# Modulation blocks of a conditioned decoder layer: eight products on TensorE against weighed sums on VectorE

## What is computed

```python
cond = jax.nn.silu(c)                                  # 1024 values
mod = (cond @ w_ada[l] + b_ada[l])[:, None, :]         # w_ada: 1024 x 6144
sh_m, sc_m, g_m, sh_f, sc_f, g_f = jnp.split(mod, 6, axis=-1)
h = modulate(rms_norm(x, norm_mix_g[l]), sh_m, sc_m)
x = x + g_m * hybrid_mixer(h, w_in[l], ...)            # w_in: 1024 x 7168, w_out: 1024 x 1024
h = modulate(rms_norm(x, norm_ffn_g[l]), sh_f, sc_f)
y = moe_ffn(h, router_w[l], router_b[l], w_gate_up[l], b_gate_up[l], w_down[l], b_down[l])
x = x + g_f * y
return rms_norm(x, final_norm_g)
```

## Time and profile before

| | us |
|---|---|
| median of 3 runs | 1220.74 (1220.02 to 1222.51) |
| profiled execution | 1220.39 |
| its span, first to last instruction | 1218.6 |
| mean granted TensorE clock, share of full | 0.951 |

### The profile page before, as it was taken

One profiled execution on the slowest core, in us unless ns is written; L12 is line 12 of the kernel. 1 busy time (PEld: TensorE's weight loads), 2 busy tenths in 40 slices (PEclk: granted clock), 3 DMA queues, 4 the chain that ended last, 5 costly groups with the idle time before them and its releaser, 6 DMA issues.

```text
span 1218.6 us, 23737 instructions
## 1 busy us (share of the span) xinstructions
PE 976.9 (80%) x9347; PEld 517.7 (42%) x9348; DVE 449.8 (37%) x1115; ACT 400.4 (33%) x773; POOL 8.6 (1%) x21
## 2 busy tenths in 40 slices
PE   6999999988688888997568997568898678656565
PEld 3788989853244333443124443112443123111122
DVE  0655654654244234442123444222344224222223
ACT  1544424424233234432123334222344224222223
POOL 0200000000000000000000000000000000000000
PEclk9999999999999999999889999987999789898898
DMA  9979487789999989999998869999989999999995
GB/s 353 377 277 347 170 320 293 298 353 427 425 425 426 426 357 429 426 426 426 426 426 363 348 273 425 427 426 429 424 338 426 428 424 429 424 428 425 426 426 224
DMA packets 60354, 467.50 MB, mean 384 GB/s; under 512 B 5148, under 2 KB 6468, under 8 KB 24484
## 3 DMA queue, kind: packets, MB, share of 16 engines
q1 hardware_dynamic: 60324, 467.06, 93.0%
HBM read 466.00 MB, written 1.05 MB: 383 GB/s over the span
## 4 chain that ended last, share of the span: by engine, by line
PE 47%; DMA 25%; SPq 18%; issue 4%; DVE 4%; ACT 1%; DVEq 0%; ACTq 0%
PE B L1213 23%; DMA W<-in_w_down_dram 21%; PE B L960 15%; SPq L367 13%; SPq L369 4%; DMA W<-in_w_gate_up_dram 4%; PE B L1222 3%; PE B L980 2%; PE B L1164 1%; DVE EW L896 1%; DVE EW L899 1%; DVE EW L893 1%; DMA raw<-in_w_ada_dram 1%; ACT EW L592 1%; PE B L987 1%
## 5 line engine op out<-in xcount | busy, mean ns | idle before, releaser
L1213 PE MATMUL B<-W,mT 128*32 128x256 f32 (+1 forms) x5888 | 550.5, 518 | 150.8 <-DMA W<-in_w_gate_up_dram 113.5
L1213 PEld LDWEIGHTS B<-W,mT 128*32 128x32 f32 x5888 | 213.7, 113 | 458.6 <-DMA W<-in_w_gate_up_dram 177.4
L602 ACT ACTIVATE hT<-hT 32x256 bf16<-32x256 bf16 x368 | 152.6, 415 | 237.4 <-DVE hT L913 229.5
L893 DVE TENSOR_SCALAR EW<-B 128x256 f32<-128x256 f32 x46 | 19.5, 424 | 419.6 <-PE B L1213 419.6
L592 ACT ACTIVATE EW<-EW 128x256 f32<-128x256 f32 x46 | 19.2, 417 | 365.5 <-DVE EW L893 365.5
L960 PE MATMUL B<-hh,wh 128*128 128x256 f32 x384 | 110.0, 286 | 0.0
L960 PE MATMUL B<-hl,wh 128*128 128x256 f32 x384 | 108.7, 283 | 0.0
L960 PE MATMUL B<-hh,wl 128*128 128x256 f32 x384 | 108.7, 283 | 0.0
L675 DVE TENSOR_TENSOR wl<-raw,wh 128x2048 fp32r<-128x2048 f32 x32 | 72.8, 2313 | 72.7 <-ACT wh L487 72.7
L1222 PE MATMUL B<-b_gu,mT 128*32 128x512 f32 x368 | 50.5, 601 | 59.7 <-issue 48.4
L487 ACT ACTIVATE wh<-raw 128x2048 fp32r<-128x2048 f32 x32 | 59.6, 1907 | 111.7 <-DMA raw<-in_w_in_dram 76.9
(11 more groups left out here) (216 smaller groups left out, 728.2 us busy)
## 6 DMA issues: line engine op xcount, KB each, us to landing
W<-in_w_gate_up_dram SPq DMA_DIRECT2D x128, 2048.0 KB, 32.6
W<-in_w_down_dram SPq DMA_DIRECT2D x63, 2048.0 KB, 25.5
raw<-in_w_in_dram SPq DMA_DIRECT2D x13, 2048.0 KB, 8.8
raw<-in_w_ada_dram SPq DMA_DIRECT2D x12, 2048.0 KB, 12.2
raw<-in_w_out_dram SPq DMA_DIRECT2D x2, 2048.0 KB, 9.9
raw<-in_w_in_dram SPq DMA_DIRECT2D x2, 1024.0 KB, 11.5
W<-in_w_down_dram SPq DMA_DIRECT2D x2, 1024.0 KB, 38.8
x_sb<-in_x_dram SPq DMA_DIRECT2D x1, 1024.0 KB, 5.0
```

Source lines behind the costliest of these rows:

```text
L602: A(ys[CAP * m:CAP * m + CAP, g * QC:(g + 1) * QC], yp[CAP * g:CAP * g + CAP, m, :], ACT.Copy).then_inc(y_moved, 1)
L1213: t = M(o, src[:, k % KQ, CAP * (k // KQ):CAP * (k // KQ) + CAP], w, start=(first and k == 0), stop=(k == KT - 1))
```

## The change

Blocks i = 1 and 2 (eight of them) leave TensorE. VectorE multiplies each with its condition values, one per partition, and adds it up in a new tile `weighed` (128 x 4 x 512): two instructions per block, a tensor_scalar or scalar_tensor_tensor and a scalar_tensor_tensor. `weigh(1 + h, n)` stands behind the work on bank 0 of section n, and its end is what `ada_used` now counts for these units. TensorE then sums over the partitions with a tile of ones, four matmuls (`sum_weighed`) per half, behind the second spatial step of section U_; `cond` is overwritten with ones after the opening. The fourth opening block goes to the place of `wh[1]`, which is unused then, and is issued without a wait; the ring's places shift by one behind it, so that the first expert units land in other places; ScalarE's first split into `wh[1]` waits for that block's use. The filler transposes ahead of the second opening block are gone.

```diff
+        weighed = sb("weighed", [P, 4, HALF])
...
-        PLACE = (1, 2, 8, 0, 3, 4, 5, 6, 7, 9)
+        PLACE = (0, 1, 8, 2, 3, 4, 5, 6, 7, 9)
...
+        ASIDE = 3
+
+        def place(n):
+            return n if n < ASIDE else n - 1
+
         def raw_slot(n):
-            return raw[:, (n % RING) * UW:(n % RING + 1) * UW]
+            if n == ASIDE:
+                return slot(5)
+            return raw[:, (place(n) % RING) * UW:(place(n) % RING + 1) * UW]
+
+        def landed(n):
+            if n == ASIDE:
+                return s_aside, 16
+            return s_slot[place(n) % RING], 16 * (place(n) // RING + 1)
...
             for n, (kind, s, h) in enumerate(units):
-                if n >= RING:
-                    m = n - RING
+                if n != ASIDE and place(n) >= RING:
+                    m = n - RING if n - RING > ASIDE else n - RING - 1
...
             split_high(0, (1,))
+            act.wait_ge(ada_used, 4)
             split_high(1)
...
-                dve.wait_ge(ada_used, 4 * (i + 1))
+                if i == 0:
+                    dve.wait_ge(ada_used, 4)
+                else:
+                    dve.wait_ge(ada_summed, i)
...
             add_bias(0)
+            V.memset(cond[:, 0, :], 1.0).then_inc(ones_ready, 1)
...
+            def weigh(i, q):
+
+                n = unit_no[("ada", i, q)]
+                dve.wait_ge(*landed(n))
+                if q == 0 and i > 1:
+                    dve.wait_ge(ada_summed, i - 1)
+                w = raw_slot(n).rearrange("p (k j n) -> p k j n", k=2, j=4)
+                if q == 0:
+                    step(V.tensor_scalar(weighed[:, :, :], w[:, 0], cT[:, 0:1], None, ALU.mult))
+                else:
+                    step(V.scalar_tensor_tensor(weighed[:, :, :], w[:, 0], cT[:, 2 * q:2 * q + 1], weighed[:, :, :], ALU.mult, ALU.add))
+                V.scalar_tensor_tensor(weighed[:, :, :], w[:, 1], cT[:, 2 * q + 1:2 * q + 2], weighed[:, :, :], ALU.mult, ALU.add).then_inc(ada_used, 1)
+                dve.wait_ge(ada_used, 4 * i + q + 1)
+                if q == 3:
+                    dve.nop().then_inc(weighed_ready, 1)
...
+                        if b == 0 and n < 4:
+                            weigh(1 + h, n)
...
+            def sum_weighed(i):
+
+                if i == 1:
+                    pe.wait_ge(v_gelu, TA * NH)
+                    pe.wait_ge(ones_ready, 1)
+                if i == 2:
+                    pe.wait_ge(mod_ready, 2)
+                pe.wait_ge(weighed_ready, i)
+                for j in range(4):
+                    t = M(B[7][32 * j:32 * j + 32, :], cond[:, 0, :], weighed[:, j, :], start=True, stop=True)
+                t.then_inc(ada_summed, 1)
...
             for q in range(1, 4):
-                keep_warm(WARM_LOAD, B[5])
+                if q > 1:
+                    keep_warm(WARM_LOAD, B[5])
                 modulation(0, q)
...
-                        if b == 0 and i < 4:
-                            modulation(1 + h, i)
                     if s == U_:
                         spatial(2 * h + 1)
+                        sum_weighed(1 + h)
```

More of the change, by code:

```diff
@@ L221, in hybrid_trunk @@
         ranks = B[4][:, 0:3 * E]
-        s_x = sem("s_x"); s_rows = sem("s_rows"); s_bada = sem("s_bada"); s_bada_rest = sem("s_bada_rest"); s_first = sem("s_first"); s_gffn = sem("s_gffn")
+        s_x = sem("s_x"); s_rows = sem("s_rows"); s_bada = sem("s_bada"); s_bada_rest = sem("s_bada_rest"); s_first = sem("s_first"); s_aside = sem("s_aside"); s_gffn = sem("s_gffn")
         s_ws = sem("s_ws"); s_bs = sem("s_bs"); s_lng = sem("s_lng"); s_rw = sem("s_rw")
@@ L227, in hybrid_trunk @@
         s_slot = [sem(f"s_slot{n}") for n in range(RING)]
-        ada_used = sem("ada_used"); split_h = sem("split_h"); split_l = sem("split_l")
+        ada_used = sem("ada_used"); weighed_ready = sem("weighed_ready"); ada_summed = sem("ada_summed"); ones_ready = sem("ones_ready"); split_h = sem("split_h"); split_l = sem("split_l")
         c_ident = sem("c_ident"); c_iota = sem("c_iota"); c_pcol = sem("c_pcol"); c_late = sem("c_late"); pool_step = sem("pool_step")
@@ L338, in _ @@
                     sp.dma_start(dst[:, 0:k, :], src[:, 0:k, :]).then_inc(s_first, 16)
-                    sp.dma_start(dst[:, k:KT, :], src[:, k:KT, :]).then_inc(s_slot[n % RING], 16)
+                    sp.dma_start(dst[:, k:KT, :], src[:, k:KT, :]).then_inc(landed(n)[0], 16)
                 else:
-                    sp.dma_start(dst, src).then_inc(s_slot[n % RING], 16)
+                    sp.dma_start(dst, src).then_inc(landed(n)[0], 16)
                 if n == ada_units[3]:
@@ L369, in load @@
                     sp.dma_start(unit_slot(u).rearrange("p (g n) -> p g n", g=2), dn_v[e, j - NQ]).then_inc(s_unit[u % SLOTS], 16)
-            assert [n % RING for n in (NU - 3, NU - 2, NU - 1)] == [1, 2, 0]
+            assert [place(n) % RING for n in (NU - 3, NU - 2, NU - 1)] == [0, 1, 2]
             sp.wait_ge(split_l, SPLITS * (len(split_units) - 2))
@@ L483, in split_high @@
                     else:
-                        act.wait_ge(s_slot[n % RING], 16 * (n // RING + 1))
+                        act.wait_ge(*landed(n))
                     if j >= 2 and c == 0:
@@ L950, in arrived @@
             def arrived(n):
-                pe.wait_ge(s_slot[n % RING], 16 * (n // RING + 1))
+                pe.wait_ge(*landed(n))
             def split_ready(j, k):
@@ L970, in modulation @@
                     pe.wait_ge(cond_ready, 1)
[L971 to L974, removed]
                 n = unit_no[("ada", i, q)]
@@ L1301 @@
     from concourse.bass_utils import run_bass_kernel_spmd as _run
-    nc = _bacc.Bacc("TRN2", target_bir_lowering=False, num_devices=1)
+    nc = _bacc.Bacc("TRN2", target_bir_lowering=False, num_devices=1, dynamic_dma_scratch_size=2048)
     arrays, args = {}, []
```

## The result

The changed kernel takes 1268.72 us (median of 4 runs, 1267.71 to 1269.77) against 1221.45 before (4 runs, 1220.02 to 1222.51): 1.0388 times, 95% interval 1.037 to 1.0406. It is 47.3 us slower. The prediction was 1265.6 us, with 1254 to 1280 as its range.

A forecast was written before the change was run, and what follows sets the result against it. TensorE was taken to bound the mixer before, a closed round through VectorE after. 1220.4 us (profiled execution) + 45.2 (eight weighings, six landings and TensorE's 12.9 us gain included) = 1265.6 us, range 1254 to 1280.

The forecast's parts named there:

- The forecast's mechanism: In the mixer, weighing, landing, split and section work form a closed round without TensorE; mixer 45.2 us late; 80%.
- The opening, 0 us: Before the mixer's sections, early load and removed filler gain 0 us with the channel full; other bound 2.6 us.
- The instructions: On VectorE, tensor_scalar takes 1.4 us and scalar_tensor_tensor 2.3 (1.9 to 2.5); weighings 35.7 us in all.
- The transfers: In the mixer's rounds, each block lands 7.7 us after issue; landings of 9 us would add 8 us.
- The rounds: In each half of the mixer, 22.5 us to GATE_A and 23.1 to U, where TensorE needs 11.7.
- TensorE's waits: Ahead of SC_B, GATE_A, U: 7.9, 10, 10.6 us in the first half; 2.0, about 10, 10 in the second.
- ScalarE's waits: ScalarE's waits for w_in transfers would be near 100 us instead of 54.8.
- The clock: TensorE's clock falls in waits of 8 to 10 us; it can cost only behind U, at most 1.9 per half.
- The +4 us of the upper bound: Allowance for TensorE's lower clock behind U, at most 1.9 us per half.
- Behind the mixer: The expert part, a full stream of transfers, is unchanged and only shifts with the mixer's end.
- upper bounds: Additions to the forecast: +2.8 us for VectorE's instructions, +8 for landings, +4 for the clock; given as up to 1279.
- this rival: Mixer landings lengthen to 12 us because a modulation block goes first: 1292.6 us, less the clock's loss 1280; 8%.

The follow-up runs named there:

- e3: Changed kernel with each weighing ahead of the bank-0 work of its section instead of behind it; 1260.81 us, 1.0334 of the kernel before.
- e4: Changed kernel with the ring's three places divided, two for in and out blocks, one for later modulation blocks, and issues reordered; 1214.05 us, 0.9954 of before.
- e2: Changed kernel with both weighing instructions cut to 32 of 2048 columns, all waits kept; 1234.18 us (other router values), mixer's end 23.6 us later than before.
- e1: Changed kernel with the eight later blocks back on TensorE, keeping early load, shifted places and missing filler; 1219.24 us, 0.9991 of before.
- e6: Divided ring of e4 with two weighings per half moved, issues adapted and the ones-product behind GATE_B; 1209.14 us, 0.9905 of before.
- e8: Changed kernel with weighings only: old ring places, old opening load and filler transposes back; 1268.77 us, 1.0399 of before.
- e7: Changed kernel with 64 filler transposes in TensorE's waits ahead of SC_B, GATE_A and U (not SC_B of the second half); 1270.72 us, 1.042 of before.

## Why the prediction was right, step by step

**The forecast's mechanism.** It was right: e3 changes nothing but VectorE's order, e4 nothing but the places and the order of the issues, and they move the time by 8 and 55 us; e2 shows rounds that stay long without the work.

**The opening, 0 us.** It was about 1 us: ScalarE's first split came at 31.64 instead of 32.67. The first weighing began at 78.11, forecast 78.9. By the rule that the prediction took from the Trainium skill ("DMA: Bandwidth & Descriptors", section "Rules for kernel authors") it would have been up to 2.6 us; with the DMA share at 1.03, most of that didn't come.

**The instructions.** tensor_scalar 1.28 us (taken 1.4), scalar_tensor_tensor 2.35 (taken 2.3). The 1227 ns that the Trainium skill gives for the first ("VectorE: DVE Perf Modes", section "The perf-mode tier table") was nearer than the value drawn from the layer norm's row.

**The transfers.** 8.0, 8.3 and 8.1 us in the first half, 7.9, 7.9 and 8.1 in the second, instead of 7.7. This term was too small by 0.2 to 0.6 us in each, over the six by some 2 us. That is as much as the forecast was short of at the mixer's end. There, 0.05 us too little in each of the 14 scalar_tensor_tensor (0.7 in all) and the 0.8 us by which the first weighing came early about cancel, which is luck.

**The rounds.** 23.1 and 23.6 us in the first half (forecast 22.5 and 23.1), 22.6 and 23.6 in the second. TensorE's waits: 50.2 us in six, forecast 7.9 + 10 + 10.6 + 2.0 + 10 + 10.6 = 51.1. GATE_B began at 157.03 and 256.91, forecast 156.25 and 255.05. The mixer ended 47.2 us later, forecast 45.2. (TensorE's step to U also holds 0.9 us of spatial work, which the sum leaves out; it only shortens the wait.)

**ScalarE's waits.** Forecast near 100 us, measured 125.6 in 11. This number has no working beside it. Ahead of five of the splits ScalarE waited 15 to 20 us, 92.5 us together, and the shorter waits come on top.

**The clock.** It fell as forecast. The 96 products of U took 14.17 us instead of 12.5 (11.7 and the wait of 0.8), and the reason why this costs next to nothing held: TensorE is through at 155.12, and VectorE's last work on the spatial bank ends at 154.8.

```profile
154.14 0.68 DVE L779 TENSOR_TENSOR tmp<-B,tmp 128x512 f32<-128x512 f32 x1
```

So the clock cost 0.3 us in this half; in the second, TensorE waits 0.2 us for the same instruction. The +4 us of the upper bound weren't needed. One reading was too simple: the prediction has the clock at 40 us fall after a wait of 1.85 us, but with waits of 2.1 us at the same place it fell neither in e1 nor in the changed kernel.

**Behind the mixer.** Nothing was expected to change. In the profiled executions, from the last addition to x_sb to the span's end it is 969.1 us before, 971.2 now, 971.8 in e3, 971.2 in e6, but 969.6 in e8, the one with the old places, and 969.8 in e7, which has the new. So the changed kernel's profiled execution, 1269.77 us, has 2 us from here beside the 2 us of the mixer, and is 4.2 above the forecast; the median of 1268.72 is 3.1 above. Whether the expert part pays 1 to 2 us for the new places stays open.

**The sums.** Two slips in the prediction change nothing above. Its upper bounds added up give 1280.4 us, not 1279; and landings of 12 us are 4.3 us longer than 7.7, not 4.5, so that this rival would have given 1291.4.

## What to carry to other kernels

When work moves to an engine with room, look at its queue, not at its share: what it does before the new work, what buffer the new work frees, and whether anything behind it in the same queue waits for a transfer into that buffer. If so, the round's length (work, transfer, conversions) stands against the bound engine's step, and here it was 23 us against 11.7 with no engine full. Leaving out nearly all of the new work gave back only half of the loss (e2). What cured it was a buffer whose next content isn't needed by the same queue (e4): with that, the same instructions gave a gain of 0.5%, and of 0.95% with two weighings moved as well (e6).

## What the runs showed of the hardware

A transfer of 2 MB into a channel that had been idle took 7.7 to 8.6 us from issue to landing, and 9.0 and 9.2 us in two cases of e7. So a place that is freed only when its next content is due costs that time each round.

The granted clock of TensorE fell from 1.00 to its lower level (0.50, 1.2 GHz) in each of the changed kernel's five waits of 8.7 to 10.7 us, and was back 4 to 6 us after the products resumed. Bringing it back to 0.97 and 0.95 with filler transposes (e7) brought nothing, since TensorE wasn't what the rest waited for. Around the shorter wait ahead of the first product at 38 us, it fell in some executions and not in others with the same instructions up to there (e7, wait 2.0 us: fell; changed kernel, wait 2.15 us: didn't).
